# Weights' raw and low parts moved by 64 bytes in SBUF, in a two-block transformer kernel on one core

## Chip, cores and metric

The kernel runs on one core of one Trainium2 chip. The metric is the device time of one execution in microseconds; the median of 3 runs is given, with lowest and highest.

## What is computed

The reference runs 256 tokens of width 1024 through two models in a row, in float32. The first has two layers of feed-forward, a mixer of four gated branches (two convolutions, sliding-window attention, forgetting attention), and feed-forward again. The second has four layers, each a mixer (differential attention, HGRN2, a chunked spatial gating unit, differential attention), cross attention to 256 memory tokens, and feed-forward. Cut to the part in which most of the time goes:

```
def _swiglu(x, w_gate, w_up, w_down):
    return (jax.nn.silu(x @ w_gate) * (x @ w_up)) @ w_down
...
for l in range(DEPTH):                      # 2
    x = x + 0.5 * _swiglu(_rmsnorm(x, ffn1_norm[l]), ...)      # D = 1024, D_FF = 2816
    z = _rmsnorm(x, mix_norm[l]) @ w_in[l]
    ...
    x = x + merged @ w_out[l]
    x = x + 0.5 * _swiglu(_rmsnorm(x, ffn2_norm[l]), ...)
```

## The kernel before

All weights are cut on the host into 460 units of 128 x 2048 float32 (1 MiB): a column unit is 256 columns of a 1024-row matrix, a row unit 256 rows of a 1024-column one. A feed-forward stage has 33 units, and there are eight such stages; the other 196 units belong to mixers and cross attention.

Each product of an activation and a weight is made of three matmuls in the single-pass format fp32r. Both operands are cut into a high part (rounded to fp32r) and a low part (the rest), and low x high, high x low and high x high are added. The units pass through a ring of 5 slots of 8192 bytes a partition. SyncE loads slot `j` of `raw` when TensorE has finished the unit that was there; ScalarE makes the high part `wh` from `raw` (L1077); GpSimd makes the low part and writes it over `raw` (L399; `wl` is a second name for the memory of `raw`, in fp32r):

```
pool.tensor_tensor(wl[:, j * UW:(j + 1) * UW], raw[:, j * UW:(j + 1) * UW],
                   wh[:, j * UW:(j + 1) * UW].bitcast(F32), ALU.subtract)
```

TensorE then takes the unit in 16 steps of three matmuls (`product`, L447 to L453). For features in the rows of the output the weights are the stationary operand and 256 tokens of activations stream:

```
for k, (sh, sl, vh, vl) in enumerate(parts):
    pe.matmul(out, sl, vh, start=start and k == 0, stop=False, **kw)      # L450
    pe.matmul(out, sh, vl, start=False, stop=False, **kw)                 # L451
    ins = pe.matmul(out, sh, vh, start=False, stop=stop and k == len(parts) - 1, **kw)   # L452
```

Here `sh`, `sl` are 128 columns of `wh`, `wl` and `vh`, `vl` are 256 columns of the activations' high and low parts (`ah`, `al`; in other stages `mh`, `ml`, `gh`, `gl`, `oh`, `ol` and others). For tokens in the rows (`tokens`) the roles are swapped: 128 columns of activations are loaded and 256 columns of weights stream. A record `G<-ah,wl` has the streamed operand first and the loaded one second; G and S are PSUM tensors. The order of all work is written out by hand with semaphores, one queue for each engine.

The place of each tensor in SBUF is set by a running offset. `sb(name, width)` takes the next free bytes. The offset is rounded up to 64 before `raw`. A column of `product` starts at a multiple of 512 bytes in a slot and in the activations, so that the starts of two operands differ, modulo 256, by what their tensors differ. Counted from the start of `raw`, modulo 256, the kernel before has: `raw`, `wl`, `wh`, `x` at 0; `ah`, `al`, `full`, `mh`, `ml`, the parameters, the constants (`con`, of which `decays` is a part) and `ones` at 192; the work area, in which `gh`, `gl`, `oh`, `ol`, `lh`, `ll` and others lie, at 192 by this line:

```
at[0] += (raw_at + 192 - at[0]) % 256
work_at = at[0]
```

One place has operands that are equal modulo 256: in HGRN2 `exponents` streams 256 columns of `decays` against 128 of `lh` (L898) and `ll` (L899).

Of the kernel before, what the change touches and what calls it, by code (L numbers as in the profile page):

```python
# [128 lines left out]
def build(nc, w_units, params_d, consts_d, hot_d, rel_d, x_d, mem_d, ws_d, bs_d, out_d,  # L129
          table_d, units=UNITS, stop_after=None):  # L130

    at = [nc.sbuf_base]

    def sb(name, width, dt=F32, offset=None):

        if offset is None:
            offset = at[0]
            at[0] += (4 * width + 31) // 32 * 32
        return nc.alloc_sbuf_tensor_at(name, [P, width], dt, offset=offset)

    at[0] = (at[0] + 63) // 64 * 64
    raw_at = at[0]
    raw = sb("raw", RING * UW)
    wl = sb("wl", RING * UW, F32R, offset=at[0] - 4 * RING * UW)
    wh = sb("wh", RING * UW, F32R)
    x = sb("x", KD * T)
    at[0] += 192
# [2684 lines left out]
def program(nc, arrays, **kw):  # L2832
    args = [nc.dram_tensor(k, list(a.shape), F32, kind="ExternalInput").ap() for k, a in arrays.items()]
    args.append(nc.dram_tensor("out", [P, KD * T], F32, kind="ExternalOutput").ap())
    args.append(nc.dram_tensor("tables", [12, P, PERIOD], F32, kind="Internal").ap())
    build(nc, *args, **kw)
# [12 lines left out]
```

How the kernel before makes its waits and increments, by code:

```python
        @block.sync  # L364
# [8 lines left out]
                sp.dma_start(raw[:, n * UW:(n + 1) * UW], w_units[n, :, :]).then_inc(raw_landed[n], 16)  # L373
                if n == 1:
                    sp.dma_start(onehot[0:NB + 1, :], hot_d).then_inc(tables_in, 16)
                    sp.dma_start(rel[0:NB + 1, 0:12], rel_d).then_inc(tables_in, 16)
            sp.dma_start(par[:, KD:NPAR], params_d[:, KD:NPAR]).then_inc(par_rest, 16)
            sp.dma_start(con[:, :], consts_d).then_inc(consts_in, 16)
            with sp.Fori(1, units // RING) as i:
                for j in range(RING):
                    sp.wait_ge(unit_done, RING * i + (j + 1 - RING))
                    sp.dma_start(raw[:, j * UW:(j + 1) * UW], w_units[i * RING + j, :, :])\
                        .then_inc(raw_landed[j], 16)
            for c2 in range(KD // 2):
                sp.wait_ge(result, c2 + 1)
                sp.dma_start(out_d[:, 512 * c2:512 * (c2 + 1)], full[:, 512 * c2:512 * (c2 + 1)])\
                    .then_inc(stored, 16)
            sp.wait_ge(stored, 16 * (KD // 2))
# [2 lines left out]
        @block.gpsimd  # L394
# [1 line left out]
            def low(n, j):  # L396
                pool.wait_ge(high_ready, n + 1)
                pool.tensor_tensor(wl[:, j * UW:(j + 1) * UW], raw[:, j * UW:(j + 1) * UW],
                                   wh[:, j * UW:(j + 1) * UW].bitcast(F32), ALU.subtract)\
                    .then_inc(low_ready, 1)
            pool.wait_ge(low_ready, 2)
            for j in range(2, RING):
                low(j, j)
```

## Time and profile before

| | |
|---|---|
| median of 3 runs | 2921.4 us (2918.1 to 2921.99) |
| profiled execution | 2919.41 us, its span 2917.4 us |
| mean granted TensorE clock | 0.987 |
| TensorE busy | 2848.8 us, 98% of the span, 24180 matmul records |
| GpSimd, ScalarE, VectorE busy | 72%, 45%, 37% |

The span goes from the first to the last instruction. Matmul records overlap, since each has a start, the streaming and the way out of the array, so that the busy time of TensorE is a union, and the distance between two starts is what a matmul costs. A window's count holds each record of which any part lies in the window.

### The profile page before, as it was taken

The page shows a single profiled execution, that of the slowest core. Times are in us where ns is not written, and L with a number is a line of the kernel's source. Part 1 is how long each engine was busy: PE and PEld are TensorE (multiplying, and loading weights), DVE is VectorE, ACT ScalarE, POOL GpSimd, SP SyncE. Part 2 cuts the span into 40 slices and gives each one's busy share as a digit, 9 for nine tenths or more (in the row PEclk, how much of TensorE's full clock was granted, in tenths as well). Part 3 has the DMA queues.
Part 4 walks back from the last instruction along what each step waited for, and adds up shares of the span by engine and source line. Part 5 has one row for each costly group of instructions (what it writes and reads, how often), then busy time and mean ns, then how long its engine had stood idle before and what let it go on. Part 6 is the DMA issues. An engine that isn't in the chain of part 4 may idle for free.

```text
span 2917.4 us, 55892 instructions
## 1 busy us (share of the span) xinstructions
PE 2848.8 (98%) x24180; PEld 2798.8 (96%) x24180; DVE 1074.1 (37%) x1883; ACT 1325.1 (45%) x1476; POOL 2108.9 (72%) x462
## 2 busy tenths in 40 slices
PE   8999999999999999999999999999999999999998
PEld 8999889999998899999999998999998999999998
DVE  4317444223165343245333135333134331353331
ACT  5344534344345454345443474543354433454432
POOL 6887558878876578876688783668786588666784
PEclk9999999999999899999999999999999999999999
DMA  8964335555554255554455542445554455544553
GB/s 229 209 209 154 136 124 185 188 186 193 197 180 146 105 201 183 184 180 145 145 188 188 188 175 73 156 163 188 188 189 159 146 187 188 175 155 148 183 185 109
DMA packets 74197, 496.88 MB, mean 170 GB/s; under 512 B 8399, under 2 KB 13135, under 8 KB 14968
## 3 DMA queue, kind: packets, MB, share of 16 engines
q1 hardware_dynamic: 68344, 485.88, 46.5%
q10 hardware_dynamic: 5632, 7.62, 2.5%
q8 instruction: 191, 3.13, 0.4%
q14 instruction: 30, 0.25, 0.0%
HBM read 490.05 MB, written 3.41 MB: 169 GB/s over the span
## 4 chain that ended last, share of the span: by engine, by line
PE 86%; POOL 3%; issue 3%; DVE 3%; DMA 3%; ACT 2%; SPq 0%; POOLq 0%; DVEq 0%; ACTq 0%
PE G L450 21%; PE G L451 21%; PE G L452 21%; PE S L450 6%; PE S L451 6%; PE S L452 6%; POOL wl L399 3%; DMA raw<-w_units 3%; PE G L656 1%; PE S L1006 1%; ACT wh L1077 1%; PE S L531 1%; PE S L805 0%; PE S L768 0%; PE S L762 0%
## 5 line engine op out<-in xcount | busy, mean ns | idle before, releaser
L399 POOL TENSOR_TENSOR wl<-raw,wh 128x2048 fp32r<-128x2048 f32 x458 | 2108.7, 4616 | 778.0 <-ACT wh L1077 757.0
L1077 ACT ACTIVATE wh<-raw 128x2048 fp32r<-128x2048 f32 x456 | 873.0, 1917 | 1086.5 <-DMA raw<-w_units 1086.3
L450 PE MATMUL G<-ah,wl 128*128 128x256 f32 x4304 | 1214.3, 282 | 12.0 <-DVE wl L1724 8.6
L451 PE MATMUL G<-al,wh 128*128 128x256 f32 x4304 | 1207.3, 281 | 0.0
L452 PE MATMUL G<-ah,wh 128*128 128x256 f32 x4304 | 1206.6, 280 | 0.0
L450 PEld LDWEIGHTS G<-ah,wl 128*128 128x128 f32 x4304 | 824.3, 192 | 20.1 <-issue 15.2
L452 PEld LDWEIGHTS G<-ah,wh 128*128 128x128 f32 x4304 | 815.9, 190 | 0.0
L451 PEld LDWEIGHTS G<-al,wh 128*128 128x128 f32 x4304 | 815.4, 189 | 0.4
L450 PE MATMUL S<-gh,wl 128*128 128x256 f32 x1408 | 395.0, 281 | 3.7 <-POOL wl L399 3.7
L451 PE MATMUL S<-gl,wh 128*128 128x256 f32 x1408 | 394.7, 280 | 0.0
L452 PE MATMUL S<-gh,wh 128*128 128x256 f32 x1408 | 394.6, 280 | 0.0
L450 PEld LDWEIGHTS S<-gh,wl 128*128 128x128 f32 x1408 | 268.7, 191 | 4.1 <-issue 4.1
L452 PEld LDWEIGHTS S<-gh,wh 128*128 128x128 f32 x1408 | 265.7, 189 | 0.0
L451 PEld LDWEIGHTS S<-gl,wh 128*128 128x128 f32 x1408 | 265.2, 188 | 0.0
L1877 DVE TENSOR_TENSOR G<-G,root 128x512 f32<-128x512 f32 x88 | 61.5, 699 | 368.2 <-PE G L452 368.2
L1915 DVE SCALAR_TENSOR_TENSOR S<-S,x 128x512 f32<-128x512 f32 x28 | 19.6, 700 | 372.4 <-PE S L452 370.9
L1875 DVE TENSOR_TENSOR G<-G,root 128x512 f32<-128x512 f32 x88 | 61.5, 698 | 192.2 <-PE G L452 191.9
L450 PE MATMUL G<-mh,wl 128*128 128x256 f32 x384 | 107.7, 281 | 3.1 <-DVE ml L2076 2.5
L450 PE MATMUL G<-wh,al 128*128 128x256 f32 x384 | 107.1, 279 | 1.1 <-DVE ll L2518 1.1
L452 PE MATMUL G<-wh,ah 128*128 128x256 f32 x384 | 106.6, 278 | 0.0
L451 PE MATMUL G<-wl,ah 128*128 128x256 f32 x384 | 106.6, 278 | 0.0
L450 PE MATMUL G<-oh,wl 128*128 128x256 f32 x384 | 106.5, 277 | 0.0
(367 smaller groups left out, 3787.5 us busy)
## 6 DMA issues: line engine op xcount, KB each, us to landing
raw<-w_units SPq DMA_DIRECT2D x459, 1024.0 KB, 4.8
bias<-tables ACTq DMA_DIRECT2D x24, 128.0 KB, 3.1
tables<-trow ACTq DMA_DIRECT2D x12, 192.0 KB, 9.1
con<-consts SPq DMA_DIRECT2D x1, 1056.0 KB, 16.9
x<-x_in SPq DMA_DIRECT2D x4, 256.0 KB, 5.6
raw<-w_units SPq DMA_DIRECT2D x4, 256.0 KB, 6.1
memx<-mem_in ACTq DMA_DIRECT2D x1, 1024.0 KB, 7.5
out<-full SPq DMA_DIRECT2D x4, 256.0 KB, 2.5
```

What stands on the lines that cost most here:

```text
L399: pool.tensor_tensor(wl[:, j * UW:(j + 1) * UW], raw[:, j * UW:(j + 1) * UW], wh[:, j * UW:(j + 1) * UW].bitcast(F32), ALU.subtract)\
L450: pe.matmul(out, sl, vh, start=start and k == 0, stop=False, **kw)
L451: pe.matmul(out, sh, vl, start=False, stop=False, **kw)
L452: ins = pe.matmul(out, sh, vh, start=False, stop=stop and k == len(parts) - 1, **kw)
L531: ins = pe.matmul(out[:, 0:T], ones[:, 0:P], full[:, k * T:(k + 1) * T], start=k == 0, stop=k == 1)
L656: ins = pe.matmul(out, v_of(kc), pt[:, kc * 512 + n * P:kc * 512 + (n + 1) * P], start=kc == 0, stop=kc == nk // P - 1)
L1006: ins = pe.matmul(out[:, h * T:(h + 1) * T], qf[:, f * T + g * P:f * T + (g + 1) * P], kc[:, f * T:(f + 1) * T], start=dc == 0, stop=dc == 1)
L1077: act.activation(wh[:, j * UW:(j + 1) * UW], raw[:, j * UW:(j + 1) * UW], ACT.Copy)\
L1875: dve.tensor_tensor(pairs(gate), pairs(gate), along, ALU.mult).then_inc(scaled, 1)
L1877: dve.tensor_tensor(pairs(value), pairs(value), along, ALU.mult).then_inc(up_scaled, 1)
L1915: dve.scalar_tensor_tensor(xs if last else held[k], held[k], factor, xs, ALU.mult, ALU.add)\
```

## The change

The raw weights (and so the low parts, which share their memory) begin 64 bytes further, and 192 bytes are put behind them, so that the high parts, and all that follows, keep their place modulo 256; everything from `wh` on lies 256 bytes further. `raw_at`, from which the place of the work area is worked out, is taken ahead of the 64 bytes and stays. No instruction is added, taken away or moved on any engine. In the changed kernel the lines behind the diff have numbers higher by 2.

```
     at[0] = (at[0] + 63) // 64 * 64
     raw_at = at[0]
+    at[0] += 64
     raw = sb("raw", RING * UW)
     wl = sb("wl", RING * UW, F32R, offset=at[0] - 4 * RING * UW)
+    at[0] += 192
     wh = sb("wh", RING * UW, F32R)
     x = sb("x", KD * T)
     at[0] += 192
```

| modulo 256 from the old start of `raw` | before | now |
|---|---|---|
| `raw`, `wl` | 0 | 64 |
| `wh`, `x` | 0 | 0 |
| activations, constants, work area | 192 | 192 |
| activations less `wl` | 192 | 128 |
| activations less `wh` | 192 | 192 |

## Rows read from the trace of the kernel before

**Rows 1.** The page: busy time of two engines, the chain that ended last by engine
```profile
PE 2848.8 (98%) x24180; PEld 2798.8 (96%) x24180; DVE 1074.1 (37%) x1883; ACT 1325.1 (45%) x1476; POOL 2108.9 (72%) x462
...
PE 86%; POOL 3%; issue 3%; DVE 3%; DMA 3%; ACT 2%; SPq 0%; POOLq 0%; DVEq 0%; ACTq 0%
```

**Rows 2.** Waits of TensorE: for whom, us in total, times, longest
```profile
PE S L450 <- POOL wl L399: 3.7, 2, 3.5
```

**Rows 3.** The page, groups by line: shapes, count, busy us, mean ns, idle before
```profile
L399 POOL TENSOR_TENSOR wl<-raw,wh 128x2048 fp32r<-128x2048 f32 x458 | 2108.7, 4616 | 778.0 <-ACT wh L1077 757.0
...
L450 PE MATMUL G<-ah,wl 128*128 128x256 f32 x4304 | 1214.3, 282 | 12.0 <-DVE wl L1724 8.6
L451 PE MATMUL G<-al,wh 128*128 128x256 f32 x4304 | 1207.3, 281 | 0.0
L452 PE MATMUL G<-ah,wh 128*128 128x256 f32 x4304 | 1206.6, 280 | 0.0
```

**Rows 4.** Windows, TensorE, in the eight feed-forward stages: us, busy (count), clock, DMA
```profile
40.00:138.00 98.00, 98.00 (x867) 1.00 0.90 202
464.00:576.00 112.00, 112.00 (x953) 1.00 0.52 188
653.00:758.00 105.00, 105.00 (x929) 1.00 0.54 194
1193.00:1250.00 57.00, 57.00 (x486) 1.00 0.51 184
1489.00:1598.00 109.00, 109.00 (x928) 1.00 0.52 187
1949.00:2060.00 111.00, 111.00 (x945) 1.00 0.52 186
2324.00:2433.00 109.00, 109.00 (x927) 1.00 0.52 187
2730.00:2841.00 111.00, 111.00 (x944) 1.00 0.53 188
```

**Rows 5.** Groups of 464:576, 653:758, 1708:1726 and 1733:1754 us, one each
```profile
L450 PE MATMUL G<-ah,wl 128*128 128x256 f32 x317 | 89.1, 281 | 0.0
...
L450 PE MATMUL G<-ah,wl 128*128 128x256 f32 x310 | 85.6, 276 | 0.0
...
L450 PE MATMUL G<-wh,al 128*128 128x256 f32 x54 | 14.9, 276 | 0.0
...
L450 PE MATMUL G<-wh,al 128*128 128x256 f32 x60 | 16.7, 279 | 0.0
```

**Rows 6.** Windows, TensorE, in mixers and cross attention, as in rows 4
```profile
400.00:427.00 27.00, 27.00 (x232) 1.00 0.44 157
434.00:460.00 26.00, 26.00 (x232) 1.00 0.53 184
1708.00:1726.00 18.00, 18.00 (x161) 1.00 0.55 192
1676.00:1705.00 29.00, 29.00 (x259) 1.00 0.51 182
1733.00:1754.00 21.00, 21.00 (x180) 1.00 0.43 158
1830.00:1861.00 31.00, 31.00 (x266) 1.00 0.54 193
2290.00:2319.00 29.00, 29.00 (x258) 1.00 0.51 177
2697.00:2726.00 29.00, 29.00 (x258) 1.00 0.50 175
```

**Rows 7.** Timeline of TensorE in HGRN2: start us, us, line, operands; seven in a row
```profile
1764.95 0.28 PE L899 MATMUL S<-decays,ll 128*128 128x256 f32 x1
...
1765.67 0.28 PE L899 MATMUL S<-decays,ll 128*128 128x256 f32 x1
```

**Rows 8.** The chain in time order, 1415:1430 us: 32 plain fp32 matmuls
```profile
1419.41 6.91 PE S L1006 x32
```

More of the change, by code:

```diff
@@ L142, in build @@
     raw_at = at[0]
+    at[0] += 64
     raw = sb("raw", RING * UW)
     wl = sb("wl", RING * UW, F32R, offset=at[0] - 4 * RING * UW)
+    at[0] += 192
     wh = sb("wh", RING * UW, F32R)
```

## The prediction

> **What bounds the kernel now.** I read the page's busy row of TensorE first, then the groups by line, then counts of matmuls in windows. TensorE is busy 98% of the span, and the chain that ended last is TensorE for 86% of it [rows 1]. GpSimd, the next busiest, has 72% and is waited for by TensorE for 3.7 us in the whole run [rows 1, 2]. So the time is the number of matmuls times the distance from one start to the next, and only something that changes this distance can matter. The groups by line [rows 3] show where they are: three lines of `product`, one matmul each, 256 columns, three to a "triple". From the code, 460 weight units of 16 triples and 16 more (one unit in each of the two mixers of the first block is half used twice) are 7376 triples, 22128 matmuls, of the 24180 that the page counts.
>
> The mean ns of a matmul record is no distance, since records overlap. The distance comes from a window in which TensorE never pauses: (window + one record) / count. In 464 to 576 us (a feed-forward stage) that is (112 + 0.28)/953 = 117.8 ns; in 653 to 758 us it is (105 + 0.28)/929 = 113.3 ns [rows 4]. Same code, same tiles, same granted clock (1.00), same GpSimd and ScalarE work beside it. There are two rhythms and nothing between: the six slow windows of [rows 4] all give 117.8 or 117.9, the two fast ones 113.3 or 113.4. The record length tells them apart too, 281 ns against 276 [rows 5]. In cycles of the granted 2.4 GHz they are 272 for a matmul and 848 for three (282.7 each): 16 cycles over the 256 columns, and 32 more for each triple.
>
> What these surpluses look like is a disagreement between two readers of SBUF. While a matmul streams its 256 columns, the next weights (128 columns) are loaded. The second reason to think so is a third distance. The two matmuls on `decays` read both operands from addresses that are equal modulo 256 (constants and work area both 192 from the raw weights); in a run of them six distances take 1765.67 - 1764.95 = 0.72 us, 120.0 ns each, 288 cycles [rows 7]. In the 22128 matmuls of the three lines one operand is now always 64 bytes, modulo 256, from the other, and they take 113.3 or 117.8. So distance 0 costs 16 cycles more than distance 64 at its best. Nothing in the trace has one operand at 128 in this form of matmul. That is the unknown of this change.
>
> Here a page bears on it. The Trainium skill, "SBUF — State Buffer", section "Who interferes with whom", says that TensorE's two read ports (moving operand, weight load) are its own and that it never waits on anyone; by it an address can't cost anything, and the change would give 2921 us. The trace has 113.3, 117.8 and 120.0 ns for one form at one clock, which that section doesn't explain; an estimate by "TensorE: Matmul & The Clock Gate", "Back-to-back issue gap", is 256/2.4 + 2.5 = 109.2 ns, under all three.
>
> **The change, part by part.** No instruction is added, removed or moved. What moves are addresses. The tensors `raw` and `wl` go from 0 to 64 modulo 256; `wh`, `x`, activations, constants and work area keep 0, 0, 192, 192, 192. The layout is 256 bytes longer.
>
> *TensorE.* A triple is: load `wl`, stream `ah`; load `wh`, stream `al`; load `wh`, stream `ah`. The load of `wl` runs under the stream of the matmul before it (`ah`). That pair goes from 64 apart to 128 apart; the two pairs with `wh` stay at 64. Where tokens are the rows of the output the roles are swapped (the weights stream, the activations are loaded), and again one stream in three, that of `wl`, changes. So one pair in each of 7376 triples changes.
>
> Price of a changed pair, from both sides. Below: an undisturbed matmul. The plain fp32 matmuls of the cross attention run at 6.91/32 = 215.9 ns for 256 columns, 518 cycles [rows 8]: two cycles per column and 6 over. One cycle per column and the same 6 make 262 cycles, 109.2 ns, an estimate; a gain of 4.1 ns on 113.3. Above: 120.0 ns, as at distance 0 [rows 7], a loss of 6.7 ns. Over 7376 triples: -30 us to +49 us. I take 120.0. The two distances that cost least here, 64 above and 64 below (the normal roles and the swapped ones, whose records are 276 ns long in one window and 279 in another [rows 5]), are odd multiples of 64; 0 and 128 are the even ones, and the one that is measured is the dear one. It is a choice between two readings: if what matters is how far apart the two are, 128 is the best of all.
>
> *The rhythms.* With all pairs alike a run of matmuls falls into the 340.0 ns triple (3 x 113.3) or the 353.3 ns triple, and stays in it until TensorE next pauses. How much of the run is slow? In the feed-forward stages, 8 of 33 units, six of eight are slow [rows 4]: 6 x 33 x 16 = 3168 triples x 13.3 ns = 42 us. Of eight windows in the other stages 27 + 21 + 31 = 79 of 210 us are slow [rows 6], 38%; of the 7376 - 4224 = 3152 triples there that is 1186, worth 16 us. So 58 us of the present time are the slow rhythm's. The three runs of before lie 3.9 us apart, while one feed-forward stage that changes its rhythm would move the time by 528 x 13.3 ns = 7 us: each stage falls into its rhythm in every run alike, so it is set by the timing of its start, and by the addresses. A triple with two pairs at 64 and one at 128 is no longer three alike steps, and I take it that the slow rhythm, in which each triple as a whole loses 32 cycles, doesn't survive the 16 cycles that the odd pair inserts: one rhythm, 113.3 + 113.3 + 120.0 = 346.7 ns.
>
> *GpSimd and ScalarE.* Both read `raw`, and GpSimd `wh` too, until now equal modulo 256, now 64 apart. The low part takes 4.62 us [rows 3]. A unit's 48 matmuls take 48 x 113.3 = 5.44 us, so the low part would have to grow by 18% to be late; what a faster one could give back is the 3.7 us of [rows 2]. I count nothing. The cover is TensorE's own length, and it would be thinner by 0.2 us a unit in stages that become fast.
>
> *Sum.* +7376 x 6.7 ns = +49 us for the changed pair, -58 us for the slow rhythm that is gone: -9 us. The profiled execution took 2919.4 us (span 2917.4 and 2.0 around it), 2.0 under the median of 2921.4. Against the median: 2912 us.
>
> **The rivals.**
> A, distance counts and the slow rhythm goes: every triple 340.0 ns, -58 us, 2863 us; with the changed pair at 109.2 it would be 2833. For it: 0 is the worst distance and 128 the farthest from it. Against it: nothing at 128 is measured.
> B, my forecast: 2912 us, from 2900 to 2922, as a few stages may keep a slower form.
> C, the placement of `wl` against the activations does nothing, both rhythms stay where they are: 2921 us. For it: the page on SBUF named above. Against it: the 120.0 ns of [rows 7].
> D, the slow rhythm becomes the rule: the 7376 - 3168 - 1186 = 3022 triples that are fast now lose 13.3 ns each, +40 us, 2962 us. The mechanism: an unequal pair in each triple gives every run of matmuls the push that a bad start gives it now. The point from which it decides: with a changed pair that costs nothing, 5.8 us (0.2%) more are reached with 436 more slow triples, 65% of all against 59% now. For it: six of eight long stages are slow already, so the slow rhythm is the one more easily reached.
> E, the changed pair costs 6.7 ns in both rhythms, whose shares stay: +49 us, 2970 us.
> F, all three at 120.0: 147 - 58 = +90 us, 3011 us.
>
> **How the numbers follow.** A 0.17, B 0.30, C 0.13, D 0.22, E 0.13, F 0.05. The likeliest is B, 2912. The range of 8 in 10 goes from A to E, 2858 to 2970; B's own is 2900 to 2922. What can be told from no change is 0.2%, 5.8 us. Of B 0.27 is faster by more and 0.03 within it. Faster: 0.17 + 0.27 = 0.44. Same: most of C and that of B, 0.15. Slower: the rest, 0.41, which is D, E, F and a touch of C.
>
> **What would show it.** Count the matmuls in a long feed-forward window of the new trace, 112 us without a pause: 953 is the slow rhythm, 991 the fast one (A), 971 is B, 936 is F. B also shows in single starts: of three, one at 120 ns and two at 113, at the same line each time, with one number for all eight stages. Two numbers between stages speak for E (346.7 and 360.0 ns a triple) or for C and D (340.0 and 353.3, with changed shares). If the mean of the GpSimd low part moved from 4.62 us by more than 18%, or the time moved while distances in the windows stayed, my reading of what bounds the kernel would be wrong. The forecast is wrong most easily in the price at 128, which no row shows, and in the claim that an unequal triple has one rhythm only.

## The result

The changed kernel takes 2966.7 us (median of 4 runs, 2961.8 to 2968.1) against 2921.3 us of before: ratio 1.0156, 95% interval 1.0143 to 1.017, 45.4 us more. The profiled execution has a span of 2964.6 us. Forecast were 2912 us, from 2858 to 2970. The time lies in the range, near its upper end; it is slower, to which I had given 0.41.

The page of the changed kernel, busy time, the chain by engine, and the groups that answer to [rows 1, 3] (L452, L453 and L454 are now the three matmuls of `product`, L401 the low part):

```profile
PE 2901.0 (98%) x24180; PEld 2850.2 (96%) x24180; DVE 1072.7 (36%) x1883; ACT 1325.1 (45%) x1476; POOL 2100.2 (71%) x462
...
PE 87%; POOL 3%; issue 3%; DVE 2%; DMA 2%; ACT 2%; SPq 0%; POOLq 0%; DVEq 0%
...
L401 POOL TENSOR_TENSOR wl<-raw,wh 128x2048 fp32r<-128x2048 f32 x458 | 2100.0, 4597 | 833.7 <-ACT wh L1079 813.0
...
L452 PE MATMUL G<-ah,wl 128*128 128x256 f32 x4304 | 1219.6, 283 | 12.2 <-DVE wl L1726 8.8
L453 PE MATMUL G<-al,wh 128*128 128x256 f32 x4304 | 1224.7, 285 | 0.0
L454 PE MATMUL G<-ah,wh 128*128 128x256 f32 x4304 | 1220.4, 284 | 0.0
```

TensorE's busy time grew by 2901.0 - 2848.8 = 52.2 us, all of the loss and 5 us that it now waits less. GpSimd's low part is as long as before (4.60 us, 4.62 before), though `raw` and `wh` are no longer equal modulo 256. The records of all three lines grew, not those of one pair alone.

Windows of TensorE in six of the feed-forward stages, as in [rows 4] (us, busy, count, clock, DMA):

```profile
40.00:132.00 92.00, 92.00 (x780) 1.00 0.89 200
480.00:570.00 90.00, 90.00 (x763) 1.00 0.52 185
660.00:760.00 100.00, 100.00 (x848) 1.00 0.53 189
1222.00:1275.00 53.00, 53.00 (x451) 1.00 0.52 183
1520.00:1625.00 105.00, 105.00 (x891) 1.00 0.51 181
2780.00:2880.00 100.00, 100.00 (x848) 1.00 0.52 184
```

(90 + 0.28)/763 = 118.3 ns, (92 + 0.28)/780 = 118.3, (53 + 0.28)/451 = 118.1: one number in all of them, where before there were 113.3 and 117.8. (The other two feed-forward stages have it too, 354.7 ns for three, but their windows hold some other matmuls.) The two rhythms have become one, and it is slower than the slower of the two. The groups of 480 to 570 us show where it is lost:

```profile
L453 PE MATMUL G<-al,wh 128*128 128x256 f32 x254 | 71.8, 283 | 0.0
L454 PE MATMUL G<-ah,wh 128*128 128x256 f32 x254 | 71.5, 282 | 0.0
L452 PE MATMUL G<-ah,wl 128*128 128x256 f32 x255 | 71.3, 280 | 0.0
```

The records are 280 to 283 ns long; in the fast stage of before they were 276 [rows 5]. And the timeline of TensorE in the same stage, one row for each start:

```profile
499.80 0.28 PE L453 MATMUL G<-al,wh 128*128 128x256 f32 x1
499.92 0.28 PE L454 MATMUL G<-ah,wh 128*128 128x256 f32 x1
500.04 0.28 PE L452 MATMUL G<-ah,wl 128*128 128x256 f32 x1
500.15 0.28 PE L453 MATMUL G<-al,wh 128*128 128x256 f32 x1
500.27 0.28 PE L454 MATMUL G<-ah,wh 128*128 128x256 f32 x1
500.39 0.28 PE L452 MATMUL G<-ah,wl 128*128 128x256 f32 x1
500.50 0.29 PE L453 MATMUL G<-al,wh 128*128 128x256 f32 x1
```

To the 10 ns of this view no line stands out: 0.12, 0.12, 0.11, 0.12, 0.12, 0.11. The trace has whole ns, and over all starts of 470 to 570 us the mean step is 116.2 ns after L452 (load of `wh` under `ah`), 119.0 after L453, 119.5 after L454 (the changed pair: load of `wl` under `ah`). Against the fast rhythm the two pairs that were not touched lose 3 and 6 ns as well. Nor is it the slow rhythm of before: there single steps lie between 117 and 119 ns, in the fast one at 113 or 114, and here they are spread from 114 to 124.

For the whole program I take the mean of start to start three matmuls later (a triple) over all of TensorE's runs without a pause, apart for the 6736 triples whose weights are loaded ("normal") and the 640 in which they are streamed ("swapped"). Before 347.8 and 348.7 ns, now 354.7 and 353.4. 6736 x 6.9 + 640 x 4.7 = 49 us; TensorE's busy time grew by 52, the median by 45.

### The profile page after: what moved, and what is told of

Read it like the earlier page. It is cut to its first block, busy times and chain, and to the rows that moved or that the text cites. A ratio compares the mean times of both kernels' runs of the same rounds, so it can differ in the third digit from the quotient of the medians.

```text
span 2964.6 us, 55892 instructions
## 1 busy us (share of the span) xinstructions
PE 2901.0 (98%) x24180; PEld 2850.2 (96%) x24180; DVE 1072.7 (36%) x1883; ACT 1325.1 (45%) x1476; POOL 2100.2 (71%) x462
## 4 chain that ended last, share of the span: by engine, by line
PE 87%; POOL 3%; issue 3%; DVE 2%; DMA 2%; ACT 2%; SPq 0%; POOLq 0%; DVEq 0%
PE G L453 21%; PE G L452 21%; PE G L454 21%; PE S L453 6%; PE S L454 6%; PE S L452 6%; POOL wl L401 3%; DMA raw<-w_units 2%; PE G L658 1%; PE S L1008 1%; ACT wh L1079 1%; PE S L533 1%; PE S L807 0%; PE S L770 0%; PE G L830 0%
## 5 line engine op out<-in xcount | busy, mean ns | idle before, releaser
L401 POOL TENSOR_TENSOR wl<-raw,wh 128x2048 fp32r<-128x2048 f32 x458 | 2100.0, 4597 | 833.7 <-ACT wh L1079 813.0
L452 PE MATMUL G<-ah,wl 128*128 128x256 f32 x4304 | 1219.6, 283 | 12.2 <-DVE wl L1726 8.8
L453 PE MATMUL G<-al,wh 128*128 128x256 f32 x4304 | 1224.7, 285 | 0.0
L454 PE MATMUL G<-ah,wh 128*128 128x256 f32 x4304 | 1220.4, 284 | 0.0
L452 PEld LDWEIGHTS G<-ah,wl 128*128 128x128 f32 x4304 | 823.9, 191 | 20.9 <-issue 16.2
L454 PEld LDWEIGHTS G<-ah,wh 128*128 128x128 f32 x4304 | 822.4, 191 | 0.0
L453 PEld LDWEIGHTS G<-al,wh 128*128 128x128 f32 x4304 | 819.1, 190 | 0.4
L453 PE MATMUL S<-gl,wh 128*128 128x256 f32 x1408 | 397.8, 283 | 0.0
L454 PE MATMUL S<-gh,wh 128*128 128x256 f32 x1408 | 396.5, 282 | 0.0
L452 PE MATMUL S<-gh,wl 128*128 128x256 f32 x1408 | 393.7, 280 | 2.6 <-POOL wl L401 2.6
L452 PEld LDWEIGHTS S<-gh,wl 128*128 128x128 f32 x1408 | 266.2, 189 | 3.0 <-issue 3.0
L454 PEld LDWEIGHTS S<-gh,wh 128*128 128x128 f32 x1408 | 266.0, 189 | 0.0
L453 PEld LDWEIGHTS S<-gl,wh 128*128 128x128 f32 x1408 | 264.6, 188 | 0.0
L452 PE MATMUL G<-mh,wl 128*128 128x256 f32 x384 | 108.7, 283 | 1.6 <-DVE ml L2078 1.0
L453 PE MATMUL G<-ol,wh 128*128 128x256 f32 x384 | 108.5, 283 | 0.0
L453 PE MATMUL G<-ml,wh 128*128 128x256 f32 x384 | 108.4, 282 | 0.0
L452 PE MATMUL G<-wh,al 128*128 128x256 f32 x384 | 107.6, 280 | 0.8 <-DVE ll L2520 0.8
L454 PE MATMUL G<-wh,ah 128*128 128x256 f32 x384 | 108.3, 282 | 0.0
## 6 DMA issues: line engine op xcount, KB each, us to landing
con<-consts SPq DMA_DIRECT2D x1, 1056.0 KB, 16.7
```

## The experiments

Two theories stood after the result. Distance: what counts is only the distance modulo 256 between the operand that is streamed and the one that is loaded; the three distances of a triple together decide which rhythms exist. Against it, length: that the layout grew by 256 bytes (other absolute addresses), or that a low part placed otherwise than the high parts is bad wherever it lies. "Distance" in what follows is the start of the streamed operand less that of the loaded one, modulo 256; in normal triples that is 192 for all pairs before, and low 128, high 192 now.

**The length alone (ctrl256).**

```
     wl = sb("wl", RING * UW, F32R, offset=at[0] - 4 * RING * UW)
+    at[0] += 256
     wh = sb("wh", RING * UW, F32R)
```

> The kernel before with 256 bytes put between the raw weights and the high parts: every tensor from the high parts on lies 256 bytes further, as in the changed kernel, and none moves modulo 256. Distance theory (only the distance modulo 256 between the tensor that is loaded and the one that is streamed counts): 2921 us, two rhythms of 340.0 and 353.3 ns a triple in the same stages as before. Length theory (the longer layout or absolute addresses set the rhythm): near 2967 us, the 354.6 ns triple of the changed kernel.

2919.4 us against 2921.6, ratio 0.9999 (0.9978 to 1.0019). Its windows in the first three feed-forward stages:

```profile
40.00:132.00 92.00, 92.00 (x814) 1.00 0.89 213
480.00:570.00 90.00, 90.00 (x767) 1.00 0.53 187
660.00:750.00 90.00, 90.00 (x796) 1.00 0.54 198
```

113.4, 117.7 and 113.4 ns: fast, slow, fast, as in [rows 4]. The length costs nothing.

**All pairs at 128 (all128).** The padding ahead of the activations is 128 instead of 192, and so is the work area's place:

```
-    at[0] += 192
+    at[0] += 128
     acts_at = at[0]
...
-    at[0] += (raw_at + 192 - at[0]) % 256
+    at[0] += (raw_at + 128 - at[0]) % 256
```

> Activations, constants and work area at 128 instead of 192 from the weights; raw, low and high parts all at 0, so that every pair of load and stream is 128 apart. If 128 is the dear distance, as 0 is: 120.0 ns for each of 22128 matmuls, 360 ns a triple, about 2921 + 90 = 3011 us, one rhythm. If 128 is a cheap distance and only the inequality within a triple costs: 340.0 ns a triple or less, 2863 us or less. If distance doesn't matter: 2921 us.

2979.2 us against 2921.6, ratio 1.0203 (1.0165 to 1.0241). A window of its second feed-forward stage:

```profile
480.00:570.00 90.00, 90.00 (x761) 1.00 0.53 188
```

118.6 ns; over the program 356.7 ns a normal triple. None of the three numbers expected: 128 is neither as dear as 0 nor cheap. Most of the loss, though, is there already when one pair of three is at 128 (354.7).

**Maps of distances.** TensorE has two free PSUM banks behind the last result. There a kernel can run the same form of matmul at any distance, since a column of `ah` or of `wh` may start anywhere. Each case is one line of code with 48 matmuls, behind a lead-in matmul of another kind that breaks the stream:

```
             norm_sums()
+            pe.wait_ge(result, KD // 2)
+            pe.matmul(S[0][:, 0:256], ones[:, 0:128], full[:, 0:256], start=True, stop=True)
+            for i in range(48): pe.matmul(G[0][:, 0:256], wh[:, 0:128], ah[:, 16:272], start=True, stop=True)
...
```

All values are means of the steps in the last two thirds of such a line. First one distance for all (map1).

> The kernel before, and behind its last result 16 groups of matmuls of the same form (128 loaded, 256 streamed columns, high part and activations), one for each distance of stream less load from 0 to 240 bytes in steps of 16, 48 matmuls each, three times with another matmul ahead (a full one, one of 64 columns, one of 200). They write to a free PSUM bank and change no output. Distance theory: 120.0 ns from start to start at 0, 113.3 or 117.8 at 64 and 192, and what stands at 128 is the price of the changed pair. Length theory: the same number at all 16, or no order by distance.

| distance | ns a step, three lead-ins | distance | ns a step, three lead-ins |
|---|---|---|---|
| 0 | 119.6, 120.0, 120.0 | 128 | 119.9, 118.5, 118.7 |
| 16 | 116.7, 118.7, 118.6 | 144 | 118.8, 116.7, 118.8 |
| 32 | 117.8, 116.7, 117.8 | 160 | 118.5, 117.4, 120.0 |
| 48 | 118.3, 118.3, 118.3 | 176 | 119.3, 119.4, 119.2 |
| 64 | 117.8, 117.8, 117.8 | 192 | 113.3, 113.3, 117.8 |
| 80 | 120.0, 120.0, 120.0 | 208 | 119.2, 119.2, 119.2 |
| 96 | 120.0, 120.1, 120.0 | 224 | 118.3, 118.3, 118.3 |
| 112 | 113.3, 113.3, 113.3 | 240 | 117.2, 117.3, 117.2 |

There is an order, and it is not "far apart is good": 112 gives 113.3 from every lead-in, 96 and 80 give 120.0. 192 has both rhythms of [rows 4], side by side, with the same addresses and nothing else running, so neither rhythm needs the DMA or another engine. 113.3 is the least anywhere. Here the streamed operand was moved and the loaded one stayed. In map5 and map6 below it is the other way round, and at 0, 64 and 192 the same values stand: 119.6 to 120.0; 117.8; 113.3 or 117.8 (at 128 118.5 to 118.6, where map1 has 118.5 to 119.9). So the difference of the two addresses counts, not the place of one of them.

Then triples, the low part's distance apart from the high parts' (map2), in the operands of the product.

> The kernel before, and behind its last result 16 groups of triples as in the product (low part loaded, then high, high; activations high, low, high streamed), 16 triples each, the distance of stream less load 0, 64, 128 or 192 for the low part and, apart from it, for the high parts, each three times with another matmul ahead. Distance theory: low 192 and high 192 give 340.0 or 353.3 ns a triple, low 128 and high 192 give 354.6, as the changed kernel. If pairs only add up: low 128 and high 128 is three times the price of one pair of 128. If a triple has a rhythm as a whole, the mixed ones are not the sum of their pairs.

| ns a step | high 0 | high 64 | high 128 | high 192 |
|---|---|---|---|---|
| low 0 | 119.8 to 120.0 | 117.8 to 118.0 | 118.2 to 118.5 | 117.8 |
| low 64 | 117.7 to 117.9 | 117.8 | 116.8 | **113.3** |
| low 128 | 119.0 to 119.2 | 115.5 to 115.6 | 118.5 to 118.6 | **118.2** |
| low 192 | 117.8 | 118.8, 113.3, 118.8 | 117.7 to 118.7 | **113.3, 113.3, 117.8** |

The last column is the case: the kernel before is low 192, the changed one low 128. Its 118.2 x 3 = 354.5 ns is the changed kernel's triple. One row above the changed kernel's stands a placement with 113.3 from all lead-ins. Timeline rows of three of these lines, the fourth and the last of 16 starts of the first matmul of a triple, twelve triples apart: low 64 (L1098), low 128 (L1122), and the third line of low 192 (L1150):

```profile
3045.80 0.28 PE L1098 MATMUL G<-ah,wl 128*128 128x256 f32 x1
...
3049.88 0.28 PE L1098 MATMUL G<-ah,wl 128*128 128x256 f32 x1
...
3118.01 0.28 PE L1122 MATMUL G<-ah,wl 128*128 128x256 f32 x1
...
3122.27 0.28 PE L1122 MATMUL G<-ah,wl 128*128 128x256 f32 x1
...
3202.45 0.28 PE L1150 MATMUL G<-ah,wl 128*128 128x256 f32 x1
...
3206.69 0.28 PE L1150 MATMUL G<-ah,wl 128*128 128x256 f32 x1
```

4.08/12 = 340, 4.26/12 = 355, 4.24/12 = 353 ns a triple. The last two are close in length and yet not one rhythm. For the middle matmul of their triples (ns, least/median/most; the slow rhythm's records are alike, the changed placement's aren't):

```profile
L1150 PE MATMUL G<-al,wh x16: 281/281/281, 3201.5 to 3206.8; 128*128 128x256 f32 x16
...
L1122 PE MATMUL G<-al,wh x16: 279/282/286, 3117.1 to 3122.4; 128*128 128x256 f32 x16
```

**The other way with the low part (low128).** The map says to move it by 128, not by 64:

```
     raw_at = at[0]
+    at[0] += 128
     raw = sb("raw", RING * UW)
     wl = sb("wl", RING * UW, F32R, offset=at[0] - 4 * RING * UW)
+    at[0] += 128
     wh = sb("wh", RING * UW, F32R)
```

> The kernel before with raw and low parts 128 bytes further instead of 64, so that activations less low parts are 64 modulo 256 and activations less high parts stay 192. The map of triples has 113.3 ns at low 64, high 192 from all three starts, where low 192, high 192 had 117.8 from one of three. Theory of the rhythm as a whole (the three distances of a triple together set which rhythms exist): one rhythm, 340.0 ns a triple, in the 6736 triples whose weights are loaded: about 56 us less, 2865 us, up to 2872 if the 640 triples with swapped roles are slow. Theory of unequal pairs (a low part that is placed otherwise than the high parts disturbs the triple, wherever it is): near 2967 us, as the changed kernel.

2872.7 us (2869.8 to 2877.4) against 2921.4, ratio 0.9834 (0.9818 to 0.9849): 49 us faster than before, 94 faster than the change. Windows of three feed-forward stages:

```profile
40.00:132.00 92.00, 92.00 (x814) 1.00 0.89 203
480.00:566.00 86.00, 86.00 (x761) 1.00 0.54 191
1180.00:1235.00 55.00, 55.00 (x488) 1.00 0.52 185
```

113.4, 113.4, 113.3 ns, also in the second stage, which was slow in [rows 4]. Over the program 340.3 ns a normal triple and 353.4 a swapped one. A group of normal triples (480 to 566 us) and one of swapped ones (1700 to 1728 us):

```profile
L452 PE MATMUL G<-ah,wl 128*128 128x256 f32 x254 | 70.1, 276 | 0.0
...
L454 PE MATMUL G<-wh,ah 128*128 128x256 f32 x73 | 20.6, 282 | 0.0
```

6736 x -7.5 + 640 x 4.7 = -48 us. The time is at the upper end of what was expected, since the swapped triples are all slow. The theory that an odd low part is bad wherever it lies falls.

**The high parts instead (high128).** `wh` begins 64 bytes further, the padding ahead of the activations is 128: low 192, high 128.

```
     wl = sb("wl", RING * UW, F32R, offset=at[0] - 4 * RING * UW)
+    at[0] += 64
     wh = sb("wh", RING * UW, F32R)
     x = sb("x", KD * T)
-    at[0] += 192
+    at[0] += 128
```

> The other part moved: the high parts lie 64 bytes further (activations less high parts 128), raw and low parts stay 192 from the activations. Two of three pairs are at 128. Theory of the rhythm as a whole: what the map has at low 192, high 128, 353 or 356 ns a triple against 347.9 on the mean before, so 2921 + 38 to 60 us. If each pair at 128 added its own price to three equal steps, two pairs would cost twice the 49 us that the change cost: 3019 us.

2979.5 us against 2921.4, ratio 1.0196 (1.0175 to 1.0216), 356.8 ns a normal triple, where the map had 353.1 from two lead-ins and 356.1 from the third. Window 480 to 570 us:

```profile
480.00:570.00 90.00, 90.00 (x760) 1.00 0.54 187
```

Two pairs at 128 cost 58 us where one costs 45: prices of pairs don't add.

**Swapped roles and finer steps (map3, map4).**

> As the map of triples, with the roles swapped: 128 columns of activations are loaded, 256 columns of weights streamed (load al, ah, ah; stream high, low, high part), stream less load 0, 64, 128 or 192 for the low part and for the high parts. The kernel before is low 64, high 64 here, the changed one low 128, high 64. Rhythm as a whole: 113.3 or 117.8 ns at low 64, high 64, and 353.3 ns a triple (117.8 each) at low 128, high 64, the value of the changed kernel's swapped triples; low 192, high 64 tells what the other placement does there.

Low 128, high 64 (the changed kernel's): 117.7 from all three; low 64, high 64 (before): 117.8 from all three, though in the kernel some runs of these triples had 113.3; low 192, high 64 (low128's): 117.1, 117.8, 117.7; only low 192, high 192 has 113.3, from two of three. Streaming the weights and loading the activations is not the mirror of the normal roles: at high 192, low 64 gives 117.8 here and 113.3 there.

> Triples in the normal roles with the high parts at 192 and the low part at every multiple of 16 bytes. If a bank of 64 bytes is what two reads collide in, the values between 64-byte steps are near those of the nearest steps: low from 48 to 80 near 113.3 ns, from 112 to 144 near 118.2. If only one exact distance is good, 113.3 stands at 64 alone.

With high at 192, 113.3 stands at low 64 from all lead-ins and at low 192 from one; at 48 it is 117.8 and at 80 from 116.9 to 117.7. From 112 to 144 it rises from 117.8 to 118.8. The expectation for the bank theory (48 and 80 near 113.3) fails: the good distance of 64 doesn't reach 16 bytes to either side.

**Starts, places and widths (map5).**

> Behind the kernel before: triples with distances (low, first high, second high) 192/192/192, 64/192/192 and 128/192/192, each behind ten other lead-in matmuls (64 to 256 columns), then 192/128/192 and 192/192/128 behind three; then single matmuls of 256 columns with 128, 64 and 32 loaded columns at the distances 0, 64, 128 and 192. If the start chooses between rhythms that the distances allow: 192/192/192 gives 113.3 behind some lead-ins and 117.8 behind others; 64/192/192 always 113.3; 128/192/192 always 118.2. If the pair counts and not its place in the triple, the last two triples give 118.2 as well. If the surplus is the weight load's (its reads against the stream's), it shrinks with the loaded columns: at 32 the distances no longer differ and come near 109 ns. If it is something else of the stream, the widths make no difference.

| distances low/high/high | lead-ins | ns a step |
|---|---|---|
| 192/192/192 | 10 | 113.3 behind six, 117.8 behind four (the first of the six begins with 16 steps of 213 ns, at the 1.2 GHz level) |
| 64/192/192 | 10 | 113.3 behind all |
| 128/192/192 | 10 | 118.1 to 118.2 behind all |
| 192/128/192 | 3 | 118.3 |
| 192/192/128 | 3 | 118.3 to 118.4 |

Two neighbouring lines with 192/192/192, behind a lead-in of 240 columns (L1070) and one of 256 (L1072), twelve triples each:

```profile
2960.23 0.28 PE L1070 MATMUL G<-ah,wl 128*128 128x256 f32 x1
...
2964.47 0.28 PE L1070 MATMUL G<-ah,wl 128*128 128x256 f32 x1
...
2966.30 0.28 PE L1072 MATMUL G<-ah,wl 128*128 128x256 f32 x1
...
2970.39 0.28 PE L1072 MATMUL G<-ah,wl 128*128 128x256 f32 x1
```

353 and 341 ns a triple. So the distances decide which rhythms there are, and where there are two, the start chooses. The length of the lead-in isn't all of the start: these two lines have the same distances, three lead-ins each, and the one behind 256 columns is fast in map2 (L1146) and slow in map4 (L1128). What else differs was not looked for.

```profile
L1146 PE MATMUL G<-al,wh x16: 276/276/283, 3189.8 to 3194.9; 128*128 128x256 f32 x16
...
L1128 PE MATMUL G<-al,wh x16: 281/281/281, 3135.9 to 3141.2; 128*128 128x256 f32 x16
```

An odd pair costs the same in each of the three places. The widths did not do what was expected: with 64 loaded columns 113.3 or 120.0 at distance 0, 116.7 at 64 and 128, 119.0 at 192; with 32 columns 117.8, then 113.3 from two lead-ins and 120.0 from the third at 64 and 192, and 115.6, 113.3, 120.0 at 128. The surplus doesn't shrink with the load, and nothing comes under 113.3.

**The same distance with the other sign, and none (all64, all0).** As all128, with 64 and with 0 in its two places.

> Activations, constants and work area at 64 instead of 192, raw, low and high parts all at 0: the distance of each pair has the other sign. By the map single pairs at 64 have 117.8 from all three starts, and swapped triples at 192/192 mostly 113.3: 353.3 ns in 6736 triples (+5.5 us a thousand, +37 us), about 343 in 640 (-4 us), 2955 us. A theory in which only how far apart the two are counts (64 as good as 192) gives 2921 us.

> Everything at the same place modulo 256. By the map 120.0 ns from all starts, 360 ns a triple, one rhythm in every stage: 7376 x 12.1 ns = +89 us, 3011 us. The record length in windows should be 283 ns throughout.

2949.1 us against 2922.7, ratio 1.0092 (1.0075 to 1.0108), and 2998.5 us, ratio 1.0263 (1.0246 to 1.028). The windows of 480 to 570 us, all64:

```profile
480.00:570.00 90.00, 90.00 (x767) 1.00 0.52 188
```

and all0:

```profile
480.00:570.00 90.00, 90.00 (x749) 1.00 0.49 178
```

117.7 and 120.5 ns (a few other matmuls stand in the second window). Over the program 353.1 and 344.9 ns for all64, 359.9 and 359.9 for all0, each within 1 ns of what the maps say for normal triples. 64 is not as good as 192. The times are 6 and 13 us under those expected. TensorE's busy time grew by 34.3 and 88.8 us in the profiled executions, as much as the triples give (33 and 89), and it waits 4 and 3 us less there than before. Another 7 of the 13 are that the median of all0 lies under its profiled execution (3005.2 us), for a reason that no trace shows.

**Other stream lengths (map6).**

> Behind the kernel before: matmuls with 128 loaded columns and 128, 192, 256, 384 and 512 streamed columns at the distances 0, 64, 128 and 192, three lead-ins each. If the surplus belongs to each matmul (it arises while the next weights are loaded or handed over), it stays between 6 and 13 ns over one cycle per column at 256, 384 and 512 columns, as at 256 now (106.7 ns of columns against 113.3 to 120.0). If it belongs to the streamed columns (each block of them meets another reader), it doubles from 256 to 512: 13 to 27 ns over 213.3.

With 192 columns the step is 111.7 ns at every distance (the first of these lines begins at the 1.2 GHz level and has it from the 24th step on). That is 268 cycles for 192 streamed columns, so something else sets it; that it is the load of 128 columns is likely, and not shown, as no run changed the load there. With 256 it is 113.3 to 120.0, with 384 173.3 to 176.7, with 512 226.7 at 0, 228.9 at 64, 232.2 to 233.3 at 128 and 233.3 at 192. Over one cycle per column that is 16 to 32 cycles, 32 to 40, and 32 to 48: the least doubles, the most doesn't, so neither expectation holds. The order turns round, 192 from the only one with 113.3 to the worst. Two of the groups, 512 columns at distance 0 and at 192:

```profile
L1154 PE MATMUL G<-ah,wh x48: 389/389/501, 3309.0 to 3319.8; 128*128 128x512 f32 x48
...
L1172 PE MATMUL G<-ah,wh x48: 392/398/496, 3412.2 to 3423.3; 128*128 128x512 f32 x48
```

## Why the prediction was wrong, step by step

**What bounds the kernel: right.** Only the distance between starts moved the time, in eight layouts; the sum of triples gives each median to within 13 us, and TensorE's busy time to within 4.

**GpSimd and ScalarE counted at nothing: right.** The low part went from 4.62 to 4.60 us, and TensorE waits for it 2.6 us instead of 3.7.

**One rhythm instead of two: right.** Ten starts of the map at 128/192/192 and all stages of the changed kernel have one. But it is not the one that I named, 346.7 ns a triple. The 58 us that I gave to the slow rhythm are confirmed: before, the surplus over 340.0 is 6736 x 7.8 + 640 x 8.7 = 58 us, and low128, in which it is gone from the normal triples, gains 49, with 3 us lost in the swapped ones.

**"Over 7376 triples: ... I take 120.0": this is the step that failed**, and with it the addition "113.3 + 113.3 + 120.0 = 346.7". I priced the changed pair alone and left the other two at their best. The triple takes 354.7 ns: the surplus over 340 is 14.7 ns, not 6.7, and lies on all three matmuls. All pairs at 128 take 356.7, so by addition one pair would cost a third of 16.7, 5.6 ns. It costs 14.7. A triple's rhythm belongs to its three distances together; what I had was a price list of pairs with one entry measured, and that at another distance, in runs of seven.

The sum with the measured term: over the fast rhythm the changed kernel has 6736 x 14.7 + 640 x 13.4 = +108 us, where I had +49; less the 58 that is +50, where I had -9. That the loss (45) is near my +49 is a coincidence. No run shows the term as the prediction has it, 6.7 ns on one pair and nothing on the others.

**The choice between "odd multiples of 64 are cheap" and "far apart is good": both false.** 64 has 117.8 where 192 has 113.3, and 112 is as good as the best.

**"Each stage falls into its rhythm in every run alike": half right.** Seven of the eight feed-forward stages had the same rhythm in eight profiled executions of this layout (the kernel before, ctrl256 and the six maps), and the first one varied (340 to 348 ns a triple in 120 to 215 us). So did short stretches elsewhere. One of the stretches of [rows 6], in the kernel before and in map3, whose code up to there is the same:

```profile
1830.00:1858.00 28.00, 28.00 (x240) 1.00 0.50 182
...
1830.00:1858.00 28.00, 28.00 (x249) 1.00 0.53 185
```

That is 117.8 and 113.6 ns. And the kernel before ran from 2906.8 to 2928.1 us in the 13 runs beside ctrl256. My bound of 3.9 us came from three runs.

**The rivals.** D, "an unequal pair in each triple gives every run of matmuls the push", gave 2962 us, and is nearest in the length of a triple: the swapped ones are at 353.4, its number, and the normal ones 1.3 ns above. Its mechanism isn't shown: the steps are spread from 114 to 124 ns, so the runs were not pushed into the old slow rhythm but have one of their own. E's 2970 us lies nearer to the time, by luck, since no stage has its 346.7 or 360.0 ns. B and F are out by the windows: 118.3 ns is neither 115.6 nor 120.0. A was the right mechanism for the other direction of the same move: low128 is 2872.7 us where A said 2863, and the 640 swapped triples that stay slow are 9 us. C is refuted for this form of matmul: moving addresses alone gives 2873 to 2998 us. The Trainium skill, "SBUF — State Buffer", section "Who interferes with whom", says that TensorE never waits on anyone; read as in the prediction, that addresses cost nothing, it disagrees with these times, and the measurement decides.

**What stays open.** Why 113.3 is the floor, why exact distances matter, and why the load's width doesn't. The measured steps are whole or third parts of multiples of 16 cycles in many cases (272, 288, 848/3), which looks like two periodic processes that lock. That they are the two operands' reads was my reading; the dependence on their distance is shown, but the narrow loads, which should have eased it, did not. It is argued only, and why 128/192/192 in particular costs 14.7 ns stays open. An order of the three matmuls other than the present one was not tried, nor were distances other than multiples of 64 in whole kernels.

## What to carry to other kernels

When one form of instruction fills the time, measure its step in stretches without a pause, (window + record)/count, and compare stretches: two values for the same code may be a gain that is there for the taking. Don't price a placement by pairs: append the whole repeating pattern at many offsets, behind several lead-ins, to a kernel that is there already. Some 290 us behind one profiled run gave the map of triples. The normal triples of four layouts (the changed one, low128, all64, all0) lie within 0.4 ns of it, those of all128 1 ns and of high128 1 to 4 ns above. It isn't exact for everything: swapped triples at 64/64 had 353.4 in the map and 348.7 in the kernel before. And take the placement that has the low step from every start: low128 ran from 2869.8 to 2877.4 us, before from 2906.8 to 2928.1. That a step doesn't depend on the start isn't enough; all0 has that too, and is the slowest.

## What the runs showed of the hardware that was not expected

- fp32r matmuls with 128 loaded and 256 streamed columns take 113.3 to 120.0 ns from start to start at the 2.4 GHz level, by the distance of the two operands modulo 256; the whole kernel moves from 2872.7 to 2998.5 us with addresses alone.
- At one set of addresses there can be two steady rhythms, 340.0 and 353.3 ns a triple, each kept for up to 1580 matmuls; in map5 the length of the matmul ahead (240 or 256 columns) went with the choice, but 256 columns led to either one in different runs.
- At other addresses there is one rhythm from every start, and it need not be even: at 128/192/192 single steps go from 114 to 124 ns, at 64/192/192 all are 113 or 114.
- The good distance differs with the form: at 512 streamed columns 0 is best (226.7 ns) and 192 worst (233.3).
- In all maps the granted clock fell to 0.50, the 1.2 GHz level, while TensorE waited some 7 us for VectorE ahead of the first line. With lines of 256 columns it was back at 1.00 after 6.8 us. In map6, where 128 columns were streamed against 128 loaded, back to back, 213.3 ns a step, it stayed down for 140 us and rose 5 us into the first line of 192 columns. That is why those twelve lines are left out above. The window:

```profile
3020.00:3035.00 15.00, 15.00 (x71) 0.50 0.00 0
```
